# Weight buffers 64 bytes lower in SBUF, so that they start in step with the moving operands

## What is computed

```
layer 1: h = rmsnorm(x); q,k,v,f = h @ w_in        (1024 x 3080)
         8 forgetting-attention heads + 8 stick-breaking heads
         x += rmsnorm(o) @ w_out                   (1024 x 1024)
         u = causal_conv(rmsnorm(x) @ w_up)        (1024 x 5632)
         x += (silu(gate) * val) @ w_down          (2816 x 1024); x = rmsnorm(x)
layer 2: block attention, w_qkv (1024 x 3072), w_o, then SwiGLU with w_gate_up, w_down
layer 3: short convolution, w_in (1024 x 3072), w_out, then SwiGLU with w_gate_up, w_down
layers 2 and 3 scale and shift each norm by mod = silu(c) @ w_ada + b_ada  (1024 x 6144, twice)
```

## Time and profile before

| | before |
|---|---|
| median of 3 runs | 910.41 us (909.77 to 912.11) |
| the profiled execution | 912.87 us, of which the span from first to last instruction is 911.3 us |
| TensorE matmul busy | 901.9 us (99%), 7351 matmuls |
| TensorE weight load busy | 877.5 us (96%) |
| VectorE busy | 753.0 us (83%) |
| ScalarE busy | 507.5 us (56%) |
| DMA moved | 207.72 MB, mean 228 GB/s |

### The profile page before, as it was taken

The page is one execution under the profiler, slowest core; times in us unless marked ns, Lnnn a source line. Parts: engine busy times, 40 slices in busy tenths (PEclk is TensorE's granted clock), DMA queues, the critical chain, the costliest instruction groups (busy, mean ns, idle before and its releaser), DMA issues.

```text
span 911.3 us, 18262 instructions
## 1 busy us (share of the span) xinstructions
PE 901.9 (99%) x7351; PEld 877.5 (96%) x7351; DVE 753.0 (83%) x1043; ACT 507.5 (56%) x795; POOL 49.5 (5%) x87
## 2 busy tenths in 40 slices
PE   8999999999999999999999999999999999999998
PEld 8999999999999999999999999999999999999786
DVE  5998989999899799998987887987988887667544
ACT  6456747766665577664754454436554564444531
POOL 5000000000001000010000100100000000000000
PEclk9999999999999999999999999999999999999999
DMA  9887375666667948575379998884677467764541
GB/s 276 288 279 276 106 246 202 215 229 205 230 231 275 327 140 273 171 252 195 127 231 319 323 313 309 314 291 149 201 254 256 135 227 250 239 210 182 184 139 47
DMA packets 132129, 207.72 MB, mean 228 GB/s; under 512 B 4710, under 2 KB 109536, under 8 KB 126944
## 3 DMA queue, kind: packets, MB, share of 16 engines
q1 hardware_dynamic: 123968, 156.47, 51.1%
q0 software_dynamic: 8064, 50.34, 15.9%
q10 hardware_dynamic: 32, 0.01, 0.0%
HBM read 205.75 MB, written 1.05 MB: 227 GB/s over the span
## 4 chain that ended last, share of the span: by engine, by line
PE 86%; DVE 8%; ACT 4%; issue 1%; DMA 1%; SPq 0%; ACTq 0%; DVEq 0%
PE bank L1726 24%; PE bank L1728 24%; PE bank L1727 24%; DVE w_lo L1033 2%; PE bank L1883 2%; PE bank L1799 2%; PE bank L1797 2%; PE bank L1808 2%; PE bank L1771 1%; PE bank L1763 1%; PE bank L1765 1%; ACT w_hi L597 1%; DMA w_raw<-in_w_in 1%; DVE ada_acc L1049 1%; ACT prob L956 1%
## 5 line engine op out<-in xcount | busy, mean ns | idle before, releaser
L1033 DVE TENSOR_TENSOR w_lo<-w_raw,w_hi 128x1024 fp32r<-128x1024 f32 x292 | 351.7, 1221 | 105.7 <-ACT w_hi L597 103.6
L597 ACT ACTIVATE w_hi<-w_raw 128x1024 fp32r<-128x1024 f32 x291 | 304.2, 1056 | 238.2 <-PE bank L1728 220.8
L1726 PE MATMUL bank<-act_hi,w_hi 128*128 128x256 f32 x1296 | 362.2, 279 | 0.1
L1727 PE MATMUL bank<-act_lo,w_hi 128*128 128x256 f32 x1296 | 359.1, 277 | 0.0
L1728 PE MATMUL bank<-act_hi,w_lo 128*128 128x256 f32 x1296 | 359.0, 277 | 0.0
L1727 PEld LDWEIGHTS bank<-act_lo,w_hi 128*128 128x128 f32 x1296 | 244.2, 188 | 0.4 <-issue 0.2
L1726 PEld LDWEIGHTS bank<-act_hi,w_hi 128*128 128x128 f32 x1296 | 243.4, 188 | 0.7 <-issue 0.6
L1728 PEld LDWEIGHTS bank<-act_hi,w_lo 128*128 128x128 f32 x1296 | 243.4, 188 | 0.0
L1049 DVE SCALAR_TENSOR_TENSOR ada_acc<-ada_raw,silu_c,ada_acc 128x2048 f32<-128x2048 f32 (+1 forms) x56 | 114.3, 2041 | 3.6 <-DMA ada_raw<-in_w_ada 3.3
L1726 PE MATMUL bank<-hid_hi,w_hi 128*128 128x256 f32 x352 | 98.2, 279 | 0.0
L1727 PE MATMUL bank<-hid_lo,w_hi 128*128 128x256 f32 x352 | 97.2, 276 | 0.0
(11 more groups left out here) (321 smaller groups left out, 1405.5 us busy)
## 6 DMA issues: line engine op xcount, KB each, us to landing
w_raw<-in_w_gate_up SPq DMA_DIRECT2D x44, 1024.0 KB, 5.2
ada_raw<-in_w_ada POOLq DMA_DIRECT2D x40, 1024.0 KB, 5.7
w_raw<-in_w_down SPq DMA_DIRECT2D x33, 1024.0 KB, 6.5
w_raw<-in_w_in SPq DMA_DIRECT2D x23, 1024.0 KB, 6.6
w_raw<-in_w_up SPq DMA_DIRECT2D x22, 1024.0 KB, 5.7
w_raw<-in_w_qkv SPq DMA_DIRECT2D x12, 1024.0 KB, 7.0
w_raw<-in_w_out SPq DMA_DIRECT2D x8, 1024.0 KB, 7.3
ada_raw<-in_w_ada POOLq DMA_DIRECT2D x16, 512.0 KB, 4.5
```

Of the source, the lines that this page charges most:

```text
L597: act.activation(unit(w_hi, u), raw_half(c, h), ACT.Copy).then_inc(hi_ready, 1)
L1033: dve.tensor_tensor(unit(w_lo, u), raw_half(c, h), unit(w_hi, u).bitcast(F32), ALU.subtract).then_inc(lo_ready, 1)
L1726: pe.matmul(dst, a_hi, b_hi, start=start, stop=False, skip_group_check=True)
L1727: pe.matmul(dst, a_hi, b_lo, start=False, stop=False, skip_group_check=True)
```

## The change

The three small vectors are declared ahead of `w_raw` instead of behind `res`. Together they are 448 bytes, so `w_raw`, `w_hi`, `w_lo` and `res` move up by 448 bytes, which is 64 bytes down modulo 256. Everything from `act_hi` on stays at its address. The filler under `keys_w_hi` is 16 elements (64 bytes) shorter. After the change all weight tiles start at 64 modulo 256, as the moving tiles do.

```
+        mod = sb("mod", [P, 2, 6 * KT])
+        silu_c = sb("silu_c", [P, KT])
+        silu_e = sb("silu_e", [P, KT])
         w_raw = sb("w_raw", [P, RAW, 2 * UNIT])
         w_hi = sb("w_hi", [P, SPLIT, UNIT], F32R)
         w_lo = sb("w_lo", [P, SPLIT, UNIT], F32R)
         res = sb("res", [P, KT, T])
-        mod = sb("mod", [P, 2, 6 * KT])
-        silu_c = sb("silu_c", [P, KT])
-        silu_e = sb("silu_e", [P, KT])
         act_hi = sb("act_hi", [P, KT, T], F32R)
...
-        phase.enter_context(nc.sbuf_tensor("below_keys", [P, 24 * T - 48], F32))
+        phase.enter_context(nc.sbuf_tensor("below_keys", [P, 24 * T - 64], F32))
```

## The result

The changed kernel takes 942.91 us (median of 4 runs, 942.43 to 943.38), against 910.09 us (909.30 to 912.11) for the one before on the same chip. The ratio is 1.0355, 95% interval 1.0343 to 1.0368. The profiled execution took 942.43 us, its span is 940.7 us.

A forecast was written before the change was run, and what follows sets the result against it. TensorE's distance between matmul starts bounds the kernel; 5698 distances growing by 2.75 ns add 15.7 us, other edits 0, taking the profiled 912.87 us to 928.6, or 926 against the median, range 901 to 937.

The forecast's parts named there:

- What bounds the kernel: TensorE, busy 99% at full clock: time is the number of matmuls times the distance between starts, plus little.
- the offset matters: Standing against moving operand modulo 256: TensorE runs mostly fast only at +64, which the change gives up; link likely, not shown.
- Rival 1: Nothing happens: paces come from where a run locks after a break, whatever the addresses; 910 us, chance 0.22.
- (b): Products with moving weights, offset -64: 20% fast, mean distance 116.9 ns; offset 0 priced like these, +15.7 us.
- my bounds: Range of the unknown pace at offset 0: all slow 931, one step slower 959, all fast 902, no delay 869 us.
- (a): Weight-standing products of 256 columns at offset +64: 81% fast, mean distance 114.2 ns, 5698 distances.
- (c): `wf_two` at offset +160, weights of only 16 or 8 columns: 117 ns each, read as the slower pace away from +64.
- The 512-column products: Products with moving weights, whose offset goes from -64 to 0, at 228 ns: nothing put for them.
- Rival 3: Much slower: each product pays one more step, 122.4 ns; 959 us, chance 0.06.
- the 258-column rows: `raw_chunk`'s products at +64, slow or slower, median duration 283 ns; the only rows speaking for one more step.
- Rival 2: Faster: at offset 0 both reads fall in step and runs lock fast after each break; 902 us, chance 0.19.
- deep gain: A pace with none of the delay, priced from float32 transpositions at 109 ns: -41 us, 869 us, chance 0.06.

The follow-up runs named there:

- e2: Kernel before with only `w_hi`, `w_lo` and the keys' pair moved to offset 0, `w_raw` and `res` left at 128 modulo 256: 943.01 us, ratio 1.0346.
- e4: Kernel before with only `w_lo` moved to offset 0, `w_hi` and the keys' pair kept at +64: 933.29 us, ratio 1.0237.
- e6: Kernel before with all weight tiles at -64 from the moving tiles, so products with moving weights have +64: 931.01 us, ratio 1.0226.
- e7: Kernel before with all weight tiles at +128 from the moving tiles: 937.53 us, ratio 1.0299.
- e1: Computation left out: 82 bursts of 40 float32r matmuls at chosen operand offsets; 256 columns took 120.0 ns at offset 0, 113.3 or 117.8 at +64.
- experiment 6: Computation left out: matmul chains separating own offset from next weight load's; own +64, next 0 took 117.7 ns, own 0, next +64 took 118.5.

## Why the prediction was half right

It forecast 926 us, slower, at 0.53. The sign and the place are right, the size is not: 32.8 us instead of 15.7, outside the range that ended at 937.

- **What bounds the kernel** held. TensorE's pace is the time; VectorE's and ScalarE's busy times didn't move. `w_raw`, `res` and the loads, put at 0, cost 0 (e2).
- **That the offset matters** held (e2, e4, e6, e7), and Rival 1 is refuted: 3.6% for 64 bytes between the operands. The Trainium skill's rule from "SBUF — State Buffer", section "Who interferes with whom", that PE never waits on anyone, had spoken for no effect. The measurement decides against that forecast; whether the weight load and the moving read get in each other's way, no run here shows.
- **The step that failed**: "If offset 0 behaves like (b)". I priced offset 0 by the rows at -64, +2.75 ns. The kernel at -64 is e6, 931, at offset 0 943. Offset 0 has a pace of its own, 120.0 ns, which no row of before had as a steady one; my bounds stepped over it, from 117.8 (931) to 122.4 (959). 5712 distances x (119.9 - 114.2) would have been +32.6. That the time fell beyond the slow pace at all is what the sum had no term for.
- **A mis-sized term beside it**: (a) was taken as 81% fast. In two more profiles it is 91%, and the distance (a) 113.7 to 113.8 for `act`. The 15.7 us were counted from a slow draw; against the second of them (span 907.7) the changed kernel is 33.0 us longer, as the medians have it.
- **Reading (b) as the mark of -64** held in its sign: 20% fast there, 5% when the whole kernel stands at -64. But there was luck in it. I counted distances, and a stretch keeps its lock: the 81% came from a few long stretches, three of which hold two thirds of the products, so it was a handful of draws and not thousands. And the same moving-weight products at +64 (e6) are still mostly slow, 138 fast of 369. That (c) (+160, 117 ns with 16 or 8 weight columns) tells of 128 columns at +160 did not hold: the bursts gave 120.0.
- **The 512-column products**: nothing forecast, -0.5 us measured. Offset 0 is the better one for them.
- **Rival 3** (959, one more step) was nearer in kind than the forecast: another, slower pace for each product. It was argued from the 258-column rows, whose mean didn't change (120.84 and 120.76).
- **Rival 2** (faster): at offset 0 a steady pace did appear "each time after a break", but a slow one. Its threshold was off as well: with 600 of 1094 still slow, 494 x 4.4 = 2.2 us are gained and not over 2.7. The price of its deep gain came from transpositions of 128 columns; float32r takes 111.7 ns at 128 columns (e1), and no burst of 256 columns settled below 113.3.

What stays open is the mechanism. Shown: float32r has the effect and float32 has not (no other type was tried); it goes with the difference of the addresses modulo 256 where both are multiples of 16; with 128 weight columns at offset 0 the excess is 32 cycles per product at widths 256, 320, 384 and 512, but 39 at 448. That the weight load clashes with the moving read was only argued: the chains of experiment 6 contradict the simple form for either pair of reads. Why a burst at +64 has two locks, and why -64 prefers the slow one, is open as well. No version beat the kernel before.

## What to carry to other kernels

In a kernel bound by float32r matmuls, the place of the standing and moving buffers modulo 256 bytes is a parameter, worth 3.6% here. Measure bursts of 40 at each offset before laying out SBUF, several of each since the lock is drawn, and for each width and number of weight columns that the kernel uses. The best offset differs (weight columns x width: +64 for 128 x 256, 0 for 128 x 512 and 64 x 256), and at widths 128, 192 and 320 there was nothing to choose. Judge TensorE's pace by the distance between starts, not by its busy share, which was 99% in all. Where distances come in two values for the same instruction, one profile is one draw: price from several, and don't price an offset by its neighbour.

## What was not expected of the hardware

- The same matmul stream at full granted clock has locks of 113.3 and 117.8 ns at +64, chosen at a break and kept over some 510 products and more; by an estimate, 510 x 4.4 = 2.2 us, that is most of the 2.8 by which this kernel's times spread. At offset 0 there is one pace, and the changed kernel's runs spread by 1.0 us instead of 2.8.
- One weight operand of three at another offset takes the fast lock from all three products (933 us).
- A float32 matmul of 256 columns takes 432 ns, two records of 216, at every offset tried. At widths 128 and 192 float32r takes the same 111.6 to 111.8 ns as well, whatever the offset.
- The difference modulo 256 stops being all that counts below 16 bytes: +64 takes 119.8 ns instead of 113.3 with both addresses 4 bytes up.
